# The 64-key tails of both heads as one transposed tile in the window attention of an f32 encoder on one core

## What is computed

```python
cols = jnp.arange(GRID_W)                                   # 64
col_start = jnp.clip(cols - WIN_W // 2, 0, GRID_W - WIN_W)  # a window of 16
scores = einsum('bqhd,brqchd->bhqrc', q_row, k_nb) + bias
p = softmax(scores over the 8 x 16 neighbours)
out = einsum('bhqrc,brqchd->bqhd', p, v_nb) @ w_o
```

## Time and profile before

| | |
|---|---|
| Median of 3 runs | 1042.34 us (1042.2 to 1044.16) |
| Span of the profiled execution | 1041.8 us |
| TensorE busy (matmul) | 1032.3 us, 99% |
| VectorE busy | 846.8 us, 81% |
| ScalarE busy | 598.4 us, 57% |
| GpSimd busy | 103.6 us, 10% |
| Mean HBM traffic | 158 GB/s |

### The profile page before, as it was taken

One profiled execution on the slowest core, in us unless ns is written; L12 is line 12 of the kernel. 1 busy time (PEld: TensorE's weight loads), 2 busy tenths in 40 slices (PEclk: granted clock), 3 DMA queues, 4 the chain that ended last, 5 costly groups with the idle time before them and its releaser, 6 DMA issues.

```text
span 1041.8 us, 15414 instructions
## 1 busy us (share of the span) xinstructions
PE 1032.3 (99%) x6104; PEld 905.4 (87%) x6104; DVE 846.8 (81%) x1185; ACT 598.4 (57%) x836; POOL 103.6 (10%) x158
## 2 busy tenths in 40 slices
PE   9999999999999999999999999999999999999997
PEld 8888888988998998998878888889888988988985
DVE  5876688699899689688987767797799798698697
ACT  6222347665584574575765655547664674674675
POOL 3453001000000000000113000000000000000003
PEclk9999999999999999999999999999999999999999
DMA  7998568326745645633998733157056547447423
GB/s 247 375 375 300 141 165 254 108 42 207 204 132 176 177 128 177 181 97 102 372 249 249 215 90 114 55 191 274 1 122 205 163 133 202 150 134 202 147 51 111
DMA packets 36998, 182.71 MB, mean 175 GB/s; under 512 B 5760, under 2 KB 5888, under 8 KB 22848
## 3 DMA queue, kind: packets, MB, share of 16 engines
q1 hardware_dynamic: 23184, 108.57, 28.8%
q0 software_dynamic: 13456, 72.64, 28.3%
q10 hardware_dynamic: 288, 0.52, 0.2%
HBM read 136.93 MB, written 27.32 MB: 158 GB/s over the span
## 4 chain that ended last, share of the span: by engine, by line
PE 93%; DVE 4%; DMA 1%; ACT 1%; issue 1%; POOL 0%; DVEq 0%; POOLq 0%; ACTq 0%
PE bank L770 29%; PE bank L771 29%; PE bank L772 29%; DMA raw<-sevens 1%; PE bank L975 1%; PE bank L953 1%; DVE w_l L1514 1%; PE bank L938 1%; PE bank L793 1%; DVE xs L1661 1%; PE bank L997 0%; DVE big L1970 0%; ACT big L1156 0%; DVE a_l L1727 0%; ACT w_h L1128 0%
## 5 line engine op out<-in xcount | busy, mean ns | idle before, releaser
L1128 ACT ACTIVATE w_h<-big 128x1024 fp32r<-128x1024 f32 x210 | 221.7, 1058 | 216.0 <-PE bank L772 215.0
L770 PE MATMUL bank<-a_h,w_h 128*128 128x256 f32 (+1 forms) x892 | 295.0, 331 | 0.0
L772 PE MATMUL bank<-a_h,w_l 128*128 128x256 f32 (+1 forms) x892 | 292.9, 328 | 0.0
L771 PE MATMUL bank<-a_l,w_h 128*128 128x256 f32 (+1 forms) x892 | 292.8, 328 | 0.0
L1514 DVE TENSOR_TENSOR w_l<-big,w_h 128x1024 fp32r<-128x1024 f32 x210 | 252.0, 1225 | 21.8 <-ACT w_h L1128 21.8
L770 PE MATMUL bank<-w_h,hx 128*128 128x512 f32 x568 | 222.1, 391 | 0.8 <-ACT big L1376 0.4
L771 PE MATMUL bank<-w_l,hx 128*128 128x512 f32 x568 | 221.2, 389 | 0.0
L772 PE MATMUL bank<-w_h,hx 128*128 128x512 f32 x568 | 221.0, 389 | 0.0
L770 PEld LDWEIGHTS bank<-a_h,w_h 128*128 128x128 f32 x892 | 169.6, 190 | 15.8 <-issue 0.2
L772 PEld LDWEIGHTS bank<-a_h,w_l 128*128 128x128 f32 x892 | 169.6, 190 | 15.0
L771 PEld LDWEIGHTS bank<-a_l,w_h 128*128 128x128 f32 x892 | 169.6, 190 | 14.7 <-issue 0.2
(11 more groups left out here) (193 smaller groups left out, 1253.6 us busy)
## 6 DMA issues: line engine op xcount, KB each, us to landing
big<-blocks SPq DMA_DIRECT2D x56, 1024.0 KB, 5.0
big<-big POOLq DMA_DIRECT2D x30, 1024.0 KB, 7.0
raw<-weights SPq DMA_DIRECT2D x52, 512.0 KB, 6.6
raw<-t_sums SPq DMA_DIRECT2D x16, 512.0 KB, 3.7
t_sums<-sevens POOLq DMA_DIRECT2D x6, 1024.0 KB, 12.6
t_sums<-t_sums POOLq DMA_DIRECT2D x6, 1024.0 KB, 12.2
raw<-sevens SPq DMA_DIRECT2D x12, 512.0 KB, 7.8
bias_tiles<-big POOLq DMA_DIRECT2D x8, 632.0 KB, 9.3
```

Source lines behind the costliest of these rows:

```text
L770: nc.tensor.matmul(dst, sh, mh, start=start, stop=False, skip_group_check=again)
L771: nc.tensor.matmul(dst, sh, ml, start=False, stop=False, skip_group_check=again)
L772: return nc.tensor.matmul(dst, sl, mh, start=False, stop=stop, skip_group_check=again)
L1128: nc.scalar.activation(wh_all[:, w % SLOTS, :], src, ACT.Copy).then_inc(w_hi, 1)
```

## The change

For blocks 0 and 3 the tail of 64 keys is treated for both heads at once.

- The probabilities are laid out so that the two heads' tails lie beside each other in the middle of `prob` (64 columns of head 0 up to column 440, 64 of head 1 behind). One transpose makes a tile of 128 rows of them: rows 0 to 63 are head 0's tail, rows 64 to 127 head 1's. It goes to columns 384 to 511 of `tposed[0]`. A half has 7 transposes in place of 8.
- A tile `v_pair_tail` has V's tail rows for head 0 in rows 0 to 63 and in head 0's feature columns, those for head 1 in rows 64 to 127 and in head 1's feature columns, and zeros elsewhere. So one matmul of 128 by 128 adds the tails of both heads. A half has 6 values matmuls of 64 columns and one of 128 columns in place of 8 of 64 columns. The one of 128 columns comes first in half 0 and last in half 1.
- Head 1 of blocks 0 and 3 takes its chunk of 128 keys from the other end, so for that head the tail is the first (block 0) or last (block 3) 64 keys that are left.
- VectorE's copy takes 384 columns in place of 512.
- GpSimd: two memsets of 128 x 1024 in place of one of 64 x 1024. 20 copies in place of 14: for each feature half five of them after the first token half is done (`v_add` 1 or 2), five after the second (`v_add` 3 or 4). The eight copies of tails move 64 rows x 4 pieces of 64 elements (256 bytes) each, so 64 KB; the others move 128 KB as before.
- `h_raw` takes 1024 columns lower room, since `v_tile[3]` is now read by the values matmuls.

```diff
--- before.py
+++ after.py
@@ -119,6 +119,8 @@
 def part_end(s, name):
 
     return MATRIX[s][0] + 2 * MATRIX[s][1].index(name) + 2
+
+TPOSED = ((0, 0), (1, 0), (1, 1))
 
 KEYS = [(0, 24), (8, 31), (24, 31), (40, 24)]
 HALVES = [(0, 1), (3, 2)]
@@ -308,8 +310,16 @@
 
         v_tile = [big[:, 6144 + D * t:6144 + D * (t + 1)] for t in range(4)]
         v_shift = [big[:, 10240 + D * s:10240 + D * (s + 1)] for s in range(4)]
-        V_AT = [(v_tile[0], v_tile[1]), (v_shift[0], v_shift[1]), (v_shift[1], v_shift[2]),
-                (v_shift[2], v_shift[3])]
+        V_MAIN = {0: (v_tile[0], v_shift[0]), 3: (v_shift[2], v_tile[3])}
+        V_AT = {1: (v_shift[0], v_shift[1]), 2: (v_shift[1], v_shift[2])}
+
+
+        v_pair_tail = {0: big[:, 2560:3584], 3: v_shift[3]}
+        TAIL_OF = {0: (v_tile[1][0:HD, :], v_tile[0][0:HD, :]), 3: (v_tile[3][HD:P, :], v_tile[2][HD:P, :])}
+
+        def heads(t, par_):
+            return t.rearrange("p (j h f) -> p j h f", h=2, f=HD)[:, :, par_, :]
+
         q_h, q_l, k_h, k_l = (sx[:, 4096 + 512 * i:4608 + 512 * i] for i in range(4))
         prob = [big[:, 15360 + PROB_W * n:15360 + PROB_W * (n + 1)] for n in range(2)]
         probT = [big[:, 4096 + D * n:4096 + D * (n + 1)] for n in range(2)]
@@ -320,7 +330,7 @@
 
 
 
-        h_raw = big[:, 8192:10240].rearrange("p (k t) -> p k t", k=4)
+        h_raw = big[:, 7168:9216].rearrange("p (k t) -> p k t", k=4)
         s_raw = {"S1": h_raw[:, :, 0:256], "S2": h_raw[:, :, 256:512], "S4": block4(big[:, 14336:15360])}
         s3_room = s_raw["S4"]
         negated = [raw_all[:, 4 * D:6 * D]] * 2 + [big[:, 10240:12288], big[:, 12288:14336]]
@@ -403,9 +413,9 @@
             return slice(first, first + width)
 
         def prob_at(half, par_, n):
-            at = score_at(half, n)
-            offset = par_ * PROB_W // 2
-            return slice(offset + at.start, offset + at.stop)
+            width = ROWS * KEYS[HALVES[half][n]][1]
+            first = (PROB_W // 2 - width, 0)[n] if par_ == 0 else (PROB_W // 2, PROB_W - width)[n]
+            return slice(first, first + width)
 
         rows_dram = nc.dram_tensor("bias_rows", [HEADS, ROWS, 31, ROWS], f32, kind="Internal").ap()
         bias_dram = nc.dram_tensor("bias_tiles", [P, HEADS, BIAS_W], f32, kind="Internal").ap()
@@ -736,14 +746,35 @@
             t1_made(1)
             t2_stored(1)
             t2_made(1)
-            pool.memset(v_shift[3][HD:P, :], 0.0).then_inc(shift_zero, 1)
-            pool.wait_ge(v_add, 4)
+            for tail in v_pair_tail.values():
+                pool.memset(tail, 0.0).then_inc(shift_zero, 1)
+            def low_to_high(s, half):
+                f = slice(512 * half, 512 * half + 512)
+                pool.dma_start(v_shift[s][0:HD, f], v_tile[s][HD:P, f]).then_inc(v_in[half], 16)
+
+            def high_to_low(s, half):
+                f = slice(512 * half, 512 * half + 512)
+                pool.dma_start(v_shift[s][HD:P, f], v_tile[s + 1][0:HD, f]).then_inc(v_in[half], 16)
+
+            def tail_heads(b, half):
+                f = slice(512 * half, 512 * half + 512)
+                for par_ in range(2):
+                    rows = slice(HD * par_, HD * par_ + HD)
+                    pool.dma_start(heads(v_pair_tail[b][rows, f], par_), heads(TAIL_OF[b][par_][:, f], par_)).then_inc(v_in[half], 16)
+
+            pool.wait_ge(shift_zero, 2)
             for half in range(2):
-                f = slice(512 * half, 512 * half + 512)
-                for s in range(4):
-                    if s:
-                        pool.dma_start(v_shift[s - 1][HD:P, f], v_tile[s][0:HD, f]).then_inc(v_in[half], 16)
-                    pool.dma_start(v_shift[s][0:HD, f], v_tile[s][HD:P, f]).then_inc(v_in[half], 16)
+                pool.wait_ge(v_add, half + 1)
+                low_to_high(0, half)
+                high_to_low(0, half)
+                low_to_high(1, half)
+                tail_heads(0, half)
+            for half in range(2):
+                pool.wait_ge(v_add, half + 3)
+                high_to_low(1, half)
+                low_to_high(2, half)
+                high_to_low(2, half)
+                tail_heads(3, half)
             t34_made(1)
             for j in range(2, KT):
                 load_bias(j)
@@ -945,13 +976,13 @@
                 pe.wait_ge(p_ready, 2 * j + (half + 1))
                 pe.wait_ge(pt_ready, 2 * j + half)
                 pe.wait_ge(pt_ready_o, 2 * j + half)
+                tails = slice(PROB_W // 2 - HD, PROB_W // 2 + HD)
+                nc.tensor.transpose(tposed[0][:, 3 * P:4 * P], prob[half][:, tails], ident[:])
                 for par_ in range(2):
-                    for n, b in enumerate(HALVES[half]):
-                        at = prob_at(half, par_, n).start
-                        for c, (_, width) in enumerate(CHUNKS_OF[b]):
-                            t = 2 * n + c
-                            last = nc.tensor.transpose(tposed[par_][0:width, P * t:P * t + P],
-                                                       prob[half][:, at + P * c:at + P * c + width], ident[:])
+                    for t, (n, c) in enumerate(TPOSED):
+                        at = prob_at(half, par_, n).start + (P * c if n else HD * par_)
+                        width = CHUNKS_OF[HALVES[half][n]][c][1] if n else P
+                        last = nc.tensor.transpose(tposed[par_][0:width, P * t:P * t + P], prob[half][:, at:at + width], ident[:])
                 last.then_inc(t_done, 1)
 
             def values(half, j):
@@ -963,17 +994,29 @@
                         pe.wait_ge(hh_hi, j)
                     else:
                         pe.wait_ge(attn_free, j - 4)
-                    pe.wait_ge(shift_zero, 1)
-                    pe.wait_ge(v_in[j // 4], 16 * 7)
-                for n, b in enumerate(HALVES[half]):
-                    for c in range(2):
-                        for par_ in range(2):
-                            rows = slice(HD * par_, HD * par_ + HD)
-                            feats = slice(P * j + HD * par_, P * j + HD * par_ + HD)
-                            at = 512 * par_ + P * (2 * n + c)
-                            dst = attn_last if j == KT - 1 and half else attn_out
-                            last = nc.tensor.matmul(dst[rows, P * b:P * b + P], V_AT[b][c][:, feats],
-                                                    probT[half][:, at:at + P], start=c == 0, stop=c == 1)
+                    pe.wait_ge(v_in[j // 4], 16 * 10)
+                dst = attn_last if j == KT - 1 and half else attn_out
+                first = HALVES[half][0]
+
+                def tails(start):
+                    return nc.tensor.matmul(dst[:, P * first:P * first + P], v_pair_tail[first][:, P * j:P * j + P],
+                                            probT[half][:, 3 * P:4 * P], start=start, stop=not start, skip_group_check=True)
+
+                if half == 0:
+                    tails(True)
+                for t in ((0, 1, 2) if half == 0 else (1, 2, 0)):
+                    n, c = TPOSED[t]
+                    b = HALVES[half][n]
+                    for par_ in range(2):
+                        rows = slice(HD * par_, HD * par_ + HD)
+                        feats = slice(P * j + HD * par_, P * j + HD * par_ + HD)
+                        at = 512 * par_ + P * t
+                        keys = V_AT[b][c] if n else V_MAIN[b][par_]
+                        last = nc.tensor.matmul(dst[rows, P * b:P * b + P], keys[:, feats], probT[half][:, at:at + P],
+                                                start=c == 0 and (half == 1 or n == 1), stop=c == 1 or (half == 0 and n == 0),
+                                                skip_group_check=True)
+                if half == 1:
+                    last = tails(False)
                 last.then_inc(pv_done, 1)
 
             def o_step(name, k, t):
@@ -1444,8 +1487,8 @@
                 hi(W_QK + 2 * j + 7)
                 act.wait_ge(pv_done, 2 * j + 2)
                 if j < 4:
-                    act.wait_ge(v_in[0], 16 * 7)
-                    act.wait_ge(v_in[1], 16 * 7)
+                    act.wait_ge(v_in[0], 16 * 10)
+                    act.wait_ge(v_in[1], 16 * 10)
                     nc.scalar.activation(h_raw[:, j, :], attn_out[:], ACT.Copy).then_inc(raw_h, 1)
                     nc.scalar.activation(h_h[:, j, 256:512], attn_out[:, 256:512], ACT.Copy).then_inc(hh_hi, 1)
                 else:
@@ -1947,7 +1990,7 @@
 
             def evacuate(half, j):
                 dve.wait_ge(t_done, 2 * j + (half + 1))
-                nc.vector.tensor_copy(probT[half][:, 512:1024], tposed[1][:]).then_inc(pt_ready_o, 1)
+                nc.vector.tensor_copy(probT[half][:, 512:896], tposed[1][:, 0:3 * P]).then_inc(pt_ready_o, 1)
 
             def take_q(j):
                 dve.wait_ge(qk_hi, 2 * j + 1)
```

## The result

The changed kernel takes 1049.68 us (median of 5 runs, 1048.21 to 1050.36) against 1042.4 for the kernel before (5 runs, 1042.2 to 1044.16): a ratio of 1.006, interval 1.0048 to 1.0071. It is slower by about 7 us, and the forecast of 1041.9 with its range up to 1044.0 missed it. The span of the profiled execution is 1048.1 us, 6.3 longer than before. In every run that has both on record the time is 1.7 to 2.1 us above the span, so the profiled execution of before, with its span of 1041.8, would have a time of about 1043.8: one of the longer ones of its kernel. That accounts for the spans differing by 6.3 and the medians by 7.3. The later runs were made in three batches, each beside runs of the kernel before on its own chip (medians 1043.42 for e1 to e4, 1043.31 for e6 to e9, 1043.62 for e5, e10, e12 and e13), and each ratio is to those.

The account below looks back on a forecast made before the run. TensorE, busy in 99% of the span, was taken as the bound, so a pass removed there counts fully. Terms -1.75 + 0 + 1.26 + 0 - 0.1 + 0.15 = -0.44 us gave 1041.9 us, range 1040.6 to 1044.0.

Parts of the forecast that it names:

- Part 1: TensorE transposes of the probabilities: seven instead of eight in each of 16 calls, -1.75 us.
- Part 2: TensorE values matmuls: the full-width tail matmul costs what one pair costs, so 0, bounds -0.1 and +0.1 us.
- Part 3: TensorE array shape changes: 0.18 us more in each of seven head pairs, +1.26 us, bounds 0.35 and 1.54.
- Cheap changes of shape: Rival: TensorE's new split-to-full change costs only 0.09 us, total -1.35, 1041.0 us; chance 0.2.
- all free: Rival: TensorE shape changes cost nothing and the gap between values calls goes, total -2.15, 1040.2 us; chance 0.05.
- part 4: VectorE's evacuation copy shrinks from 512 to 384 columns; counted 0, at most 0.3 us gained between the values calls.
- part 5: Copies of V's earlier rows: ScalarE's wait at 573 goes, -0.1 us; one early group delays weight loads, +0.15 us uncovered.
- the early copies collide: Rival: both early groups precede the weight loads, delaying the first transposes; +0.8 us (1043.1), up to +2.4 (1044.7); chance 0.22.
- The fourth rival: TensorE runs the tail matmul at more than two steps, +3.1 us in total, 1045.4 us; chance 0.03.

Follow-up runs that it names:

- e1: Changed kernel with all 20 copies of V, in its own order, waiting for the fourth `v_add`; 1051.11 us, ratio 1.0068.
- e4: Changed kernel with the four early tail copies moved behind `v_add` 3 and 4, six whole copies still early; 1047.24 us, ratio 1.0038.
- e6: Changed kernel with all 20 copies after the fourth `v_add`, the first feature half's ten ahead of the second's; 1046.48 us, ratio 1.0028.
- e9: e7 with the tail product last in half 0 and first in half 1; 1041.62 us, one run.
- e5: Changed kernel with only the four tail transfers early, the six whole copies behind `v_add` 3 and 4; 1045.37 us, one run.
- e10: Kernel before plus two needless early DRAM transfers of 384 KB, each over 128 partitions with 3 KB rows; 1042.65 us, one run.
- e12: Kernel before with its 14 copies behind the last weight-load split, first feature half's seven first; 1043.18 us, ratio 0.9995.
- e13: Changed kernel with only the first group of five copies early, the second held until the weight loads are in; 1043.95 us, one run.
- e2: Kernel before, shapes untouched, with three whole copies per feature half sent early and four later; 1047.68 us, ratio 1.0043.
- e8: Kernel before plus six needless early DRAM transfers of 128 KB, each over 64 partitions with 2 KB rows; 1047.6 us, one run.
- e7: Changed kernel with all copies behind the last weight-load split, first feature half's ten first; 1042.42 us, ratio 0.9989.

## Why the prediction was wrong

**Held: TensorE's side.** Part 1: the transposes' row has six and one instead of eight, each step 0.109. Part 2: the tail product takes two passes of 0.11, as much as a pair; the halving of the number of matmuls brought nothing. Part 3, +0.18 a pair, is close to what the rows give: in half 1 the stage is 0.02 longer although it has a transpose less (0.11) and a gap less (0.04, below), so 0.17 went somewhere, and the changes of shape are the only new thing there. The rule of the Trainium skill on drains ("TensorEngine Tiling (Array Packing)", Key Properties) agrees with it, and e9 put a number on it. "Cheap changes of shape" and "all free" fall.

**Off by 0.04 a pair: part 4.** I left VectorE's shorter copy at 0, because ScalarE's copy stays long. The gap between the two calls of values (I had put it at 0.04 of the exit) is gone: the 24 records of L1015 run over both calls with no step above 0.11, and VectorE's copy takes 0.56 instead of 0.69. It is the upper end that I had given, -0.3 in all. So the shapes' sum is -1.75 + 1.26 - 0.3 = -0.8.

**Held: part 5, the wait at 573.** ScalarE's wait for the copies is gone (0.56, and for another reason). The extra 0.06 behind those transposes is gone too (585.12 - 584.44 = 0.68, which is 0.79 less a transpose). The covers on GpSimd held: the memsets and issues cost nobody. What follows the copies went out only 0.5 us earlier (564.85 against 565.31) and not 3, since the late `v_plus` let the last ten copies go at 559.26.

**Failed: part 5, the price of a group, and the list of places that wait for it.** Two terms were wrong, both in the same direction, and the clock was not in the sum at all.

The first is the size. I priced 512 KB of copies by bytes, at the 1.2 us per 512 KB of the earlier trace rows. That rate belongs to loads that cover all 128 partitions. By ScalarE's idle time the two groups cost 7.2 us or more instead of 2.4: 4.0 (e4) for the six whole copies, which by bytes are 1.8, and 2.5 (e5) for four tail transfers, which by bytes are 0.6. In e10, with full height, longer rows and two transfers in place of six, 768 KB cost 1.4 to 2.8, so there the byte price of 1.8 is not contradicted. In the end all of both groups went ahead of, or beside, the loads (e13: the first group alone costs 2.6), against my choice of one. The Trainium skill, "DMA: Bandwidth & Descriptors", section Queues, rings and completion order, has each engine take turns between queues; the trace agrees in that neither stream waits for the other to be empty, the loads are up to 3.4 us apart where they were 1.2. I quoted this rule and took from it which group collides, not that taking turns with slow transfers costs more than their bytes.

The second is the place. I gave the delay one cover, the 1.05 us of the earlier trace rows ahead of the transposes, where the fourth load counts. A load has a consumer on VectorE as well, and VectorE works in the order of its list: behind the split of the second load stand the maxima and the last two `v_plus`, and `scores(1, 0)` waits for these. In the trace of before, that `v_plus` ends 0.42 us ahead of the scores' start; VectorE of the kernel before:

```profile
555.47 2.36 DVE L1966 TENSOR_TENSOR big<-bank,big 128x1024 f32<-128x1024 f32 x2
```

555.47 + 2.36 = 557.83, against 558.25 in the earlier trace rows. The second wait then comes on top, since the fourth load is later than the second: TensorE stood still twice (2.7 us of the table, and some 2.9 of its 3.46 and 2.04), and not once for the longer of the two. And behind the waits the clock cost 2.6 us more, for which my sum had no term.

So the rival "the early copies collide" is what happened, and it was mis-sized: its end was +2.4, since it had bytes plus a guess for small rows, one place and no clock. Its picture of a queue that holds both groups back until the 1 MB transfer has landed doesn't fit either. In the changed kernel that transfer, issued at 537.38, took 13.0 us and landed at 550.4; the first early copy, issued at 540.38, took 8.3 and landed at 548.7, ahead of it. A late copy, issued at 559.26, took 2.8. The fourth rival fell with part 2.

**What stays open.** The clock fell in the changed kernel, e1 and e4, but not in the profiles of e2 and e8, whose two waits (2.0 and 1.9, 1.4 and 2.4) are close to those of e4 (2.1 and 1.7). It stayed at 1.00 too in e13, with one wait of 3.1. I can't say from these runs what decides it. Nor is it shown whether the copies are slow in reading, in writing, by their height, by their number or by the length of their rows: e8 and e10 differ in height, in the number of transfers (six against two) and in the rows (2 against 3 KB). e8, e10, e5, e13 and e9 are one run each.

## What to carry to other kernels

Price a transfer that moves in time by the time it holds the DMA engines, not by its bytes: look for a stretch where the same shape of transfer runs, and read the engines' share beside the GB/s. Here nearly the same bytes kept the engines busy for all of 12 us in one shape and for 0.78 of it in the other. Then list every consumer of what it delays, on each engine's own list, with its margin: a wait of 3 us arose at a place that doesn't touch the late data at all, but stands behind it in VectorE's order. And when a move is one of several edits, try the rest without it in an order that suits it: the shapes on TensorE were worth -0.8 us, and one GpSimd wait in the right place (e7) was enough to keep it.

## What the runs showed of the hardware

- A transfer over 64 partitions in rows of 2 KB delays a stream of weight loads by some twice what the same bytes do over 128 partitions in rows of 3 KB: 3.5 against 1.4 us for 768 KB (e8, e10), or 4.9 against 2.8 from the lowest undisturbed trace, with the engines at a share of 1.00 and 0.78 for 288 and 290 GB/s from 546 to 558. The number of transfers differs too. The Trainium skill, "SBUF — State Buffer", section Door 1: The DMA port swizzle, says that the bandwidth of a transfer depends on how many of the 16 ports its partitions reach, and its formula gives partitions 0 to 63, or 64 to 127, half of them. The direction agrees; that the other queue's loads suffer with it is what the runs add.
- Pieces of 256 bytes are dear beside other traffic: 256 KB in them cost the loads 2.5 us (e5), 768 KB in rows of 2 KB 4.0 (e4), so per byte 1.9 times as much (2.2 from the lowest undisturbed trace). e5 is one run, on another chip than e4.
- One round of split, full, split on the array costs 0.15 us (e9), with 128x128 passes around it.
- Behind waits TensorE can run for a while at 1.2 GHz: 2.6 us lost in the changed kernel, a granted clock of 0.64 and 0.67 in e1 from 570 to 575 and from 575 to 580, behind a wait of 7.2. It need not: the clock stayed at 1.00 in e2, e8 and e13.
